# Moving the transposes of the unrotated query and key parts from TensorE to DVE

## The reference

```python
h    = rms_norm(x, attn_norm_w)
proj = h @ w_in
hq, hf, hi, hg, c_q, c_kv, k_r = split(proj)
q    = (rms_norm(c_q) @ w_uq).reshape(B, S, 8, 128 + 64)
kv   = (rms_norm(c_kv) @ w_ukv).reshape(B, S, 8, 128 + 128)
k_nope, v = split(kv, [128])
k    = concat([k_nope, broadcast(k_r)])
q    = rope_tail(rms_norm(q, q_head_w))     # the first 128 columns are only scaled
k    = rope_tail(rms_norm(k, k_head_w))
s    = einsum('bqhd,bkhd->bhqk', q, k) * scale, block-causal mask
o_b  = softmax(s) @ v
x    = x + concat([o_a, o_b]) @ w_out
x    = x + (silu(h2 @ w_gate) * (h2 @ w_up)) @ w_down
```

## Time and profile before

| | |
|---|---|
| median of three runs | 1153.13 us |
| the profiled execution's own time | 1153.31 us |
| its span, first to last instruction | 1151.6 us |
| PE busy | 1137.8 us (99%) |
| DVE busy | 737.5 us (64%) |
| ACT busy | 575.2 us (50%) |
| granted TensorE clock | 1.000 |
| positions 36 to 98, where attention's heads are made | about 96 to 306 us of the span |

### The profile page before, as it was taken

How to read it: one execution, slowest core, us unless ns; L and a number is a source line. 1 busy time by engine, 2 the same in 40 slices (tenths; PEclk the granted TensorE clock), 3 DMA queues, 4 the chain that set the end, 5 groups by cost and what they waited for, 6 DMA issues and landing times.

```text
span 1151.6 us, 15803 instructions
## 1 busy us (share of the span) xinstructions
PE 1137.8 (99%) x5370; PEld 958.5 (83%) x5370; DVE 737.5 (64%) x1042; ACT 575.2 (50%) x817; POOL 12.0 (1%) x63
## 2 busy tenths in 40 slices
PE   7999999999999999999999999999999999999998
PEld 7988888888888888888888888888888888888887
DVE  5678787587866575657657657667667565454443
ACT  6566766668554465344344444344344343433332
POOL 3000000000000000000000000000000000000000
PEclk9999999999999999999999999999999999999999
DMA  8666454555644456666666666666666555555553
GB/s 258 186 195 191 149 169 136 160 158 162 221 161 155 166 179 183 190 197 197 185 198 194 189 198 189 196 191 193 193 191 195 190 196 197 189 199 189 194 193 135
DMA packets 113327, 213.16 MB, mean 185 GB/s; under 512 B 7001, under 2 KB 17538, under 8 KB 113026
## 3 DMA queue, kind: packets, MB, share of 16 engines
q1 hardware_dynamic: 112722, 209.44, 59.1%
q0 software_dynamic: 560, 3.15, 0.8%
HBM read 210.46 MB, written 2.10 MB: 185 GB/s over the span
## 4 chain that ended last, share of the span: by engine, by line
PE 94%; DVE 3%; ACT 1%; DMA 1%; issue 1%; SPq 0%; DVEq 0%; ACTq 0%
PE main L1251 59%; PE main L1254 30%; PE side L1374 1%; PE side L1274 1%; DVE w_lo L819 1%; DMA X<-in_x 1%; DVE hbT L1042 0%; ACT w_hi L555 0%; PE side L1362 0%; PE side L1406 0%; PE side L1321 0%; PE side L1322 0%; PE side L1308 0%; ACT junk L577 0%; PE side L1351 0%
## 5 line engine op out<-in xcount | busy, mean ns | idle before, releaser
L819 DVE TENSOR_TENSOR w_lo<-raw,w_hi 128x1024 fp32r<-128x1024 f32 (+2 forms) x400 | 478.9, 1200 | 374.6 <-ACT w_hi L555 371.7
L555 ACT CAST w_hi<-raw 128x1024 fp32r<-128x1024 f32 (+2 forms) x400 | 411.5, 1032 | 533.9 <-PE main L1251 528.0
L1251 PE MATMUL main<-w_hi,hT_hi 128*128 128x512 f32 (+2 forms) x1088 | 422.5, 389 | 0.0
L1254 PE MATMUL main<-w_hi,hT_lo 128*128 128x512 f32 (+2 forms) x1088 | 418.2, 385 | 0.0
L1251 PE MATMUL main<-w_lo,hT_hi 128*128 128x512 f32 (+2 forms) x1088 | 285.7, 385 | 0.0
L1251 PEld LDWEIGHTS main<-w_hi,hT_hi 128*128 128x128 f32 x1088 | 204.9, 188 | 38.1
L1254 PEld LDWEIGHTS main<-w_hi,hT_lo 128*128 128x128 f32 x1088 | 205.1, 189 | 37.6
L1251 PEld LDWEIGHTS main<-w_lo,hT_hi 128*128 128x128 f32 x1088 | 203.2, 188 | 38.9
L1251 PE MATMUL main<-w_hi,aT_hi 128*128 128x512 f32 x352 | 137.1, 389 | 0.0
L1254 PE MATMUL main<-w_hi,aT_lo 128*128 128x512 f32 x352 | 137.0, 389 | 0.0
L1251 PE MATMUL main<-w_lo,aT_hi 128*128 128x512 f32 x352 | 94.1, 389 | 0.0
(11 more groups left out here) (192 smaller groups left out, 549.1 us busy)
## 6 DMA issues: line engine op xcount, KB each, us to landing
raw<-in_w_gate_up SPq DMA_DIRECT2D x176, 512.0 KB, 4.5
raw<-in_w_down SPq DMA_DIRECT2D x88, 512.0 KB, 3.6
raw<-in_w_in SPq DMA_DIRECT2D x64, 512.0 KB, 3.9
raw<-in_w_out SPq DMA_DIRECT2D x32, 512.0 KB, 3.6
raw<-in_w_in SPq DMA_DIRECT2D x16, 384.0 KB, 4.6
raw<-in_w_ukv SPq DMA_DIRECT2D x8, 512.0 KB, 4.1
raw<-in_w_uq SPq DMA_DIRECT2D x8, 384.0 KB, 3.4
raw<-in_w_in SPq DMA_DIRECT2D x8, 320.0 KB, 3.1
```

The lines of the kernel that those rows point to most:

```text
L555: copy(w_hi[:, slot, 0:n], raw[:, slot, 0:n]).then_inc(s_hi, 1)
L819: tt(w_lo[:, slot, 0:n], raw[:, slot, 0:n], w_hi[:, slot, 0:n].bitcast(F32), ALU.subtract)\
L1251: m = matmul(banks[t][:, 0:cols], hi[:, at[n], tok], rhs, start=(part == "hi" and k == k_first), stop=(part == "lo" and k == k_last))
L1254: matmul(banks[t][:, 0:cols], lo[:, at[n], tok], rhs, start=False, stop=False)
```

## The change

TensorE no longer transposes the four `stage` tiles, and ACT no longer copies them: `q_t`/`k_t` keep only the two rotated tiles and use one bank instead of two. New steps `q_n`/`k_n` (j, n), n = 0 to 3, are done by DVE alone: each is four transpositions of a 32-partition strip, one from each quarter m of the tokens' partitions, written to quarter n of `qTn`/`kTn`. A query's four steps stand at four successive positions after `q_b`, a key's four at two positions, two each. `scores` waits for the last of both on a new semaphore, `s_plain`. There are 8 x 4 = 32 steps with 128 instructions.

```diff
@@ schedule()
-        s += [(q - early, ("q_a", j)), (q - 1 if early else q + 1, ("q_b", j)), (q + 4, ("q_t", j))]
+        b = q - 1 if early else q + 1
+        s += [(q - early, ("q_a", j)), (b, ("q_b", j)), (q + 4, ("q_t", j))]
+        s += [(b + 1 + n, ("q_n", j, n)) for n in range(P // Q)]
         early = j == 2
-        s += [(k - early, ("k_a", j)), (k - 1 if early else k + 1, ("k_b", j)), (k + 4, ("k_t", j))]
+        b = k - 1 if early else k + 1
+        s += [(k - early, ("k_a", j)), (b, ("k_b", j)), (k + 4, ("k_t", j))]
+        s += [(b + 1 + n // 2, ("k_n", j, n)) for n in range(P // Q)]
@@ side_uses()
     if kind in ("q_t", "k_t"):
-        return [(step + (0,), "act"), (step + (1,), "act")]
+        return [(step, "act")]
@@ new
+STAGED = [step for _, step in SCHEDULE if step[0] in ("q_b", "k_b")]
+PLAIN = [step[:2] for _, step in SCHEDULE if step[0] in ("q_n", "k_n") and step[2] == P // Q - 1]
@@ ACT
-                    plain = qTn if kind == "q_t" else kTn
-                    copy(plain[:, 2 * j:2 * j + 2, :], filled(s + (0,))[:, :].rearrange("p (h t) -> p h t", h=2))\
-                        .then_inc(s_given["act"], 1)
-                    turned = filled(s + (1,))
+                    turned = filled(s)
@@ DVE
+                elif kind in ("q_n", "k_n"):
+                    (j, n), b = a, int(kind == "k_n")
+                    dve.wait_ge(s_stage, STAGED.index((kind[0] + "_b", j)) + 1)
+                    to = (kTn if b else qTn)[Q * n:Q * (n + 1), 2 * j:2 * j + 2, :]
+                    for m in range(P // Q):
+                        tokens = stage[Q * m:Q * (m + 1), b, :, :, Q * n:Q * (n + 1)]
+                        ins = nc.vector.transpose(
+                            to.rearrange("p h (t c) -> p t h c", t=NT)[:, :, :, Q * m:Q * (m + 1)], tokens)
+                    if n == P // Q - 1:
+                        ins.then_inc(s_plain, 1)
@@ PE
-                    pe.wait_ge(s_stage, 2 * j + b + 1)
-                    ps = use(s + (0,))
-                    for h in range(2):
-                        for t in range(NT):
-                            at = h * SEQ + t * P
-                            m = transpose(ps[:, at:at + P], stage[:, b, t, h, 0:NOPE], ident[:, :])
-                    m.then_inc(s_side, 1)
-                    ps = use(s + (1,))
+                    pe.wait_ge(s_stage, STAGED.index((kind[0] + "_b", j)) + 1)
+                    ps = use(s)
...
                 elif kind == "scores":
-                    given(("k_t", h // 2, 1))
+                    given(("k_t", h // 2))
+                    pe.wait_ge(s_plain, 1 + max(PLAIN.index((x, h // 2)) for x in ("q_n", "k_n")))
```

More of the change, by code:

```diff
@@ L382, in hybrid_layer @@
         s_stage = sem("s_stage")
+        s_plain = sem("s_plain")
         s_val = sem("s_val")
@@ L982, in step @@
                     if j:
-                        dve.wait_ge(s_side, USE[(kind[0] + "_t", j - 1, 1)] + 1)
+                        dve.wait_ge(s_side, USE[(kind[0] + "_t", j - 1)] + 1)
                     if kind == "q_b":
```

## The result

The changed kernel takes 1177.62 us (median of 4 runs, 1177.19 to 1178.17); the kernel before takes 1152.89 beside it (4 runs, 1152.35 to 1153.15). The ratio is 1.0216 [1.0204, 1.0228]: 24.7 us slower, where 1175 stood in the prediction, 2.6 less. The profiled execution took 1178.17 (span 1176.5).

What follows compares the result with a forecast made beforehand. TensorE, busy 99% of the span, was taken to bound the kernel, but DVE or ACT to end each new wait: 6.6 + 1.6 + 9.9 + 4.0 = 22.1 us on 1153.3 gave 1175.4, predicted as 1175, range 1163 to 1188.

Steps and rivals of the forecast that it cites:

- four places: The insertions for pairs 0 to 3, costing 6.6, 1.6, 9.9 and 4.0 us, 22.1 us in sum.
- Three signs: Expected profile: DVE's waits before `w_lo` nearly gone, gate-bound waits none over some 3 us, TensorE idle up some 25 us.
- C: Positions 74 to 87: eight steps before gate bounds `lb_a`, 10.0 us late without slack, costing 9.9 us.
- A strip's price: One DVE transposition of a 32x128 strip: 0.31 us taken, bounds 0.225 and 0.45; a step of four 1.25 us.
- A: Positions 36 to 51, pair 0: 1.6 us late at the conversion plus 5.0 for key steps before the scan, 6.6 us.
- B: Positions 56 to 69, pair 1: query steps free; `scores` of head 2 waits for the last key strip, 1.6 us.
- D: Positions 86 to 97, pair 3: 3.75 + 5.0 - 4.7, so 4.0 us late at the probabilities of head 6.
- recovery of 4.7 us: Pair 3: DVE's waits of 1.18, 2.00 and 1.49 us behind the key steps take in 4.7 us of lateness.
- What was removed: TensorE's transposes, at most 3.5 us, and eight ACT copies, about 4.6 us: nothing counted as gained for either.
- The banks: One bank use less per pair moves every later bank; valued at nothing.
- recovery of 6.7 us: Lateness DVE was let recover at the insertions for pairs 0 and 3; without it 28 us, 1181.
- second rival: Strips dear, 0.35 to 0.45 us each, or DVE's and ACT's delays feeding on one another: 1181 to 1190; chance 0.17.

Runs made afterwards that it cites:

- Single pairs: Four kernels, each changed from the kernel before for one pair's heads only, 0 to 3: 1161.33, 1154.66, 1163.08 and 1157.13 us.
- both: Changed kernel with its strips, but TensorE's 32 transposes and both bank uses kept, their results unused: 1178.51 us, ratio 1.0219 to the kernel before.
- run of pair 0: Kernel before, with only pair 0's unrotated parts turned by DVE, at the change's positions: 1161.33 us, ratio 1.0075.
- pair 1: Kernel before, with only pair 1's unrotated parts turned by DVE, at the change's positions: 1154.66 us, ratio 1.0017.
- best_k1_back: `best` with the four steps of the key of pair 1 put back to the change's positions: 1155.27 us, ratio 1.0017 to the kernel before.
- best: Kernel before, with DVE turning keys of pairs 1 and 3, queries of pairs 0 and 1, where it waits or has slack: 1151.13 us, ratio 0.9985.
- pair1_warm: Pair 1 alone on DVE, plus 16 useless identity matmuls on TensorE ahead of `scores` of head 2: 1155.35 us, ratio 1.0023 to the kernel before.

## Why the prediction was right

**Mechanism.** The steps held: four places, each with its own price, set by which engine ends the wait, and the way out of each through DVE and ACT. Single pairs and `both` show it on the chip. Three signs that I had named came out otherwise. DVE's waits for ACT were to be nearly gone, and 22.2 of 36.1 us are left: behind a place all engines are late alike, and the next wait is there in full (3.34 us at 232.31, where it was 3.33 at 222.04 before). In C no wait was to be over some 3 us, and the one before `scores` of head 4, for ACT's copy `kTr`, is 4.39. And TensorE's idle time was to rise by some 25 us; it rose by 20.3, from 1.9 to 22.2, and the other 4.4 of the loss stand in its busy time, as matmuls at the lower clock.

**A strip's price.** My working gave 0.32 and I took 0.31, between bounds of 0.225 and 0.45. The row after says 302 ns, at a spacing of 0.315; that an elementwise row would scale a transposition this well was partly luck. A step of four adds 1.30 rather than 1.25: in A four steps add 5.2, since the scan now starts 7.46 behind the conversion (132.69 to 140.15), and before 2.28:

```profile
130.69 2.36 DVE L819 TENSOR_TENSOR w_lo<-raw,w_hi 128x1024 fp32r<-128x1024 f32 x2 [3.17 <-ACT w_hi L555]
132.97 2.43 DVE L1042 TENSOR_TENSOR_SCAN hbT<-keep,logT 128x256 f32<-128x256 f32 x4
```

In C eight add 10.4. Elementwise instructions overlap a little (two conversions start 1.14 apart and take 1.22 each), and so does the first strip here (132.69 + 1.22 is 133.91, but it starts at 133.83); the conversion behind strips does not, nor the strip at 137.59. Over the twelve steps of A's keys and of C this is 0.6 of the 2.6 us that were missing. The Trainium skill (VectorE: DVE Perf Modes, section The three transpose paths) gives 311 ns for DVE's whole 128x128 transposition in bf16. That is nearly the 302 ns which one strip of 32 partitions took here in float32. Taken as the price of one instruction the page's figure fits; but this kernel, whose blocks must change quarters, needs four instructions for each 128x128 tile.

**A, 7.2 for 6.6.** The conversion before the key steps came 2.0 late, and I had taken 1.6 out of 0 to 1.8. The eight strips twice take 5.2 in place of 5.0. In the run of pair 0 alone a fall of the clock stands on this path too, and the time is 8.6 longer.

**B, 3.1 for 1.6. This is the term that was mis-sized.** The wait for the last strip was right: 213.57 against 204.95 is 8.6, 7.2 of it from A, so 1.4 to 1.5. What I left out is what happens behind the wait: 1.6 us more are lost in the next few us, where the granted clock is 0.50. In places A, C and D the clock falls as well, but there DVE's and ACT's way sets the time, and the slower matmuls hide beside it. Of C:

```profile
263.00:266.00 3.00, 0.00 (x0) 0.00 (x0) 2.12 (x3) 2.75 (x15) 0.00 (x0) 1.00 0.52 175
266.00:269.00 3.00, 1.94 (x7) 1.76 (x8) 2.21 (x7) 2.78 (x6) 0.00 (x0) 0.52 0.00 0
269.00:273.00 4.00, 4.00 (x11) 3.15 (x10) 4.00 (x9) 0.00 (x0) 0.00 (x0) 0.51 0.56 143
273.00:276.00 3.00, 3.00 (x14) 2.45 (x14) 2.86 (x8) 1.05 (x1) 0.00 (x0) 1.00 0.43 159
```

This is the longest stretch at 1.2 GHz, some 7 us, beginning in the last microsecond of the wait of 4.39 that ends at 267.06. TensorE's lateness rises in it from 17.9 us (267.06, before 249.15) to 20.7 (274.01, before 253.27). DVE is 20.6 late all the same (282.64, before 262.00), so nothing of it is left in the end. The Trainium skill (TensorE: Matmul & The Clock Gate, section Why this matters for your kernels) warns of idle gaps between bursts of matmuls, since the clock then falls to half; the trace agrees in kind, and here a gap of 2.13 us came before such a fall. I should have weighed it in the prediction, where four waits of 1 to 5 us were forecast for a kernel whose granted clock was 1.000 throughout.

**C, 10.4 for 9.9** and **D, 4.2 for 4.0.** Eight steps at 1.30 are 10.4. In D the recovery of 4.7 us came about as forecast: the waits for ACT of 1.18, 2.00 and 1.49 before the conversions are all gone, and only one of 1.57 is left ahead of them.

**What was removed.** I counted nothing for TensorE's 3.5 us, and `both` bears that out, with a difference of 0.9 inside the intervals. Without the strips they were worth 2.0, less than the 3.1 I expected: at the scan and from 243.5 us on DVE and ACT set the time already in the kernel before, and where TensorE did, their way was close behind.

**The banks** I had valued at nothing; `both`, with the bank order of before, has the whole loss, which agrees.

**A slip in a sum.** Without the recovery of 6.7 us the second rival comes to 28.8 us and 1182, not 28 and 1181. Neither the forecast nor the range hangs on it.

## What to carry to other kernels

An engine with a third of its time idle has no general room: each instruction moved to it has to be set beside the wait in its own list that it is to fill. The same number of strips, 64, made this kernel 12.3 us slower or 1.6 faster. Before moving work off the bounding engine, find what its removal alone would give: here it was 2.0 us of the 3.5, and no placement of the strips in this order should gain more. And allow, behind any new wait of the matmul engine, for a slower clock, unless another engine sets the time there.

## What the runs showed of the hardware

- The granted clock fell to 1.2 GHz for 3.4 to 7 us at or behind single waits of TensorE between 2.1 and 4.4 us, in kernels that otherwise had 1.00 nearly all along. It is not fixed by the wait's length: 2.45 us at 117.67 in the changed kernel had none behind it, 2.42 us at 117.15 in the run of pair 0 had one.
- Where such a fall comes in some executions only and stands on the path, the time scatters. Two kernels with the wait before `scores` of head 2 spread over 2.5 us (pair 1) and 3.1 us (`best_k1_back`); `best`, without it, over 1.0; `pair1_warm`, with the wait filled, over 1.3 (10 or 11 runs each). The four runs of the changed kernel, which has this wait too, spread over only 1.0.
- A float32 matmul of the identity with itself has two records in the trace and takes 0.23 us (30 in 6.86); a transposition of the same 128x128 has one and takes 0.11 (four in 0.44).
- DVE's transposition of a strip of 32 partitions by 128 float32 columns took 302 ns, and 0.315 us from one to the next.
